# Two transformer blocks on one core: the opening norm's sums, the merged norms' signal, and work moved around waits

## What is computed

```
h = rmsnorm(x)                                   # "mix"
x = x + gated_branch_mixer(h)                    # w_in (6144 columns), conv, layernorm, pool, w_o
x = x + cross_attention(rmsnorm(x), rmsnorm(mem))
x = x + moe(rmsnorm(x))                          # 16 experts, top 2 of one group
x = rmsnorm(x)                                   # "f", end of block 1
for i in (0, 1):
    h = rmsnorm(x) * (1 + sc1) + sh1             # "n" (i = 0), "d" (i = 1)
    x = x + g1 * (nsa_mixer(h) or diff_mixer(h))
    h = rmsnorm(x) * (1 + sc2) + sh2             # "m0", "m1"
    x = x + g2 * (relu(h @ w_mlp_in)**2 @ w_mlp_out)
```

## Time and profile before

| what | value |
|---|---|
| median of 3 runs | 1421.11 us (1421.02 to 1424.01) |
| profiled execution | 1422.67 us, its span 1421.0 us |
| TensorE matmul busy | 1370.0 us, 96%, 10833 records |
| VectorE, ScalarE, GpSimd busy | 958.3, 629.1, 78.5 us |
| mean granted TensorE clock | 0.987 |
| read from HBM | 256.77 MB |

### The profile page before, as it was taken

How to read it: one execution, slowest core, us unless ns; L and a number is a source line. 1 busy time by engine, 2 the same in 40 slices (tenths; PEclk the granted TensorE clock), 3 DMA queues, 4 the chain that set the end, 5 groups by cost and what they waited for, 6 DMA issues and landing times.

```text
span 1421.0 us, 25909 instructions
## 1 busy us (share of the span) xinstructions
PE 1370.0 (96%) x10833; PEld 1306.9 (92%) x10833; DVE 958.3 (67%) x1189; ACT 629.1 (44%) x802; POOL 78.5 (6%) x131
## 2 busy tenths in 40 slices
PE   7999999999999999999999998999999987999998
PEld 6999999898899999999888578999999876999998
DVE  5569886654676767677675867888876675645553
ACT  5434435344443333333456634344445444444442
POOL 4013000000000000010100000000000000000000
PEclk9999999999899999999999999999999999999999
DMA  8565535443368887885451045999964421455551
GB/s 238 178 194 178 183 122 177 141 134 124 99 236 280 265 272 258 280 264 185 134 163 60 2 159 187 311 299 317 312 221 149 129 90 31 134 182 187 178 178 60
DMA packets 172579, 259.00 MB, mean 182 GB/s; under 512 B 5125, under 2 KB 147762, under 8 KB 172498
## 3 DMA queue, kind: packets, MB, share of 16 engines
q1 hardware_dynamic: 160890, 203.13, 44.2%
q0 software_dynamic: 10768, 53.43, 11.2%
q10 hardware_dynamic: 840, 1.28, 0.3%
HBM read 256.77 MB, written 1.05 MB: 181 GB/s over the span
## 4 chain that ended last, share of the span: by engine, by line
PE 83%; DVE 10%; ACT 3%; DMA 2%; issue 2%; ACTq 0%; DVEq 0%
PE ring L681 60%; PE acc L681 22%; DVE w_lo L1789 2%; ACT w_hi L1322 2%; DMA raw<-in_w_in_dram 1%; DVE arena L1933 1%; ACT arena L1322 1%; PE acc L1148 1%; PE ring L965 1%; DMA raw<-in_w_mlp_in_dram 1%; DVE arena L1838 0%; DMA raw<-in_w_xo_dram 0%; DVE norm L1804 0%; DMA raw<-in_diff_w_out_dram 0%; DVE stat L2337 0%
## 5 line engine op out<-in xcount | busy, mean ns | idle before, releaser
L1789 DVE TENSOR_TENSOR w_lo<-raw,w_hi 128x2048 fp32r<-128x2048 f32 (+1 forms) x191 | 437.0, 2290 | 302.4 <-ACT w_hi L1322 301.9
L681 PE MATMUL ring<-h_hi,w_hi 128*128 128x256 f32 x2088 | 602.2, 288 | 7.2 <-DVE h_lo L1853 2.6
L681 PE MATMUL ring<-h_lo,w_hi 128*128 128x256 f32 x2088 | 593.8, 284 | 0.0
L681 PE MATMUL ring<-h_hi,w_lo 128*128 128x256 f32 x2088 | 593.7, 284 | 0.0
L1322 ACT ACTIVATE w_hi<-raw 128x2048 fp32r<-128x2048 f32 (+1 forms) x191 | 363.8, 1905 | 248.6 <-DMA raw<-in_w_mlp_out_dram 70.0
L681 PEld LDWEIGHTS ring<-h_hi,w_hi 128*128 128x128 f32 x2088 | 403.4, 193 | 14.2 <-issue 10.5
L681 PEld LDWEIGHTS ring<-h_lo,w_hi 128*128 128x128 f32 x2088 | 403.5, 193 | 2.5 <-issue 2.2
L681 PEld LDWEIGHTS ring<-h_hi,w_lo 128*128 128x128 f32 x2088 | 403.3, 193 | 0.0
L681 PE MATMUL acc<-e_hi,w_hi 128*128 128x256 f32 x768 | 218.8, 285 | 0.1
L681 PE MATMUL acc<-e_lo,w_hi 128*128 128x256 f32 x768 | 217.4, 283 | 0.0
L681 PE MATMUL acc<-e_hi,w_lo 128*128 128x256 f32 x768 | 217.4, 283 | 0.0
(11 more groups left out here) (286 smaller groups left out, 1273.6 us busy)
## 6 DMA issues: line engine op xcount, KB each, us to landing
arena<-in_w_ada_dram POOLq DMA_DIRECT2D x64, 768.0 KB, 6.1
raw<-in_w_mlp_in_dram SPq DMA_DIRECT2D x32, 1024.0 KB, 5.7
raw<-in_w_mlp_out_dram SPq DMA_DIRECT2D x32, 1024.0 KB, 5.1
raw<-in_w_in_dram SPq DMA_DIRECT2D x24, 1024.0 KB, 5.3
raw<-in_w_e_gate_dram SPq DMA_DIRECT2D x16, 1024.0 KB, 5.6
raw<-in_w_e_up_dram SPq DMA_DIRECT2D x16, 1024.0 KB, 6.3
raw<-in_w_e_down_dram SPq DMA_DIRECT2D x16, 1024.0 KB, 6.4
raw<-in_diff_w_in_dram SPq DMA_DIRECT2D x12, 1024.0 KB, 5.2
```

The lines of the kernel that those rows point to most:

```text
L681: return nc.tensor.matmul(dst, lhs, rhs, start=start, stop=stop, **kw)
L1789: tt(w_lo[q % SPL][:, 0:n], raw[q % RAW][:, 0:n], w_hi[q % SPL][:, 0:n].bitcast(F32), ALU.subtract)\
```

## The change

x is loaded in two halves. ScalarE squares each half on the token rows, 1024 elements a row, with the row's sum from the same instruction; the root and VectorE's reciprocal then work on 128x2. VectorE multiplies the identity by these (two 128x128 diagonals, in blocks of MEM_T), TensorE's ones matrix spreads them over the partitions into acc[0], and VectorE copies that into the norm row. The vectors' transposes go to acc[1], the memory rows' to acc[0] to acc[3], and the ring's plan loses six uses. SyncE issues its nine vector loads between panel 0 and panel 1. ScalarE takes its first table as Sqrt and rounds panel 1 only behind the h blocks.

The norm n stands ahead of f in `NORMS`, with a buffer of its own for its scaled blocks (N_QR), and GpSimd also waits for f's sum. Further: in the last step of the sparse attention n_norm goes ahead of n_pt_odd; VectorE's last `ahead(p + 2)` of an MLP is left out, and made behind the residual in the first; the split of output panel 2 of d_o goes behind the differential attention on both engines; lambda's Exp goes between the value panels; d_out squares before it copies; the Sqrt table and both last splits come before the last d_out; VectorE makes the low parts of d_o's operand between the head scalings, and ScalarE waits for the scaling's own signal instead of a small copy; d_o's first panel goes block by block. Five fillers' counts are changed.

```diff
@@ -236,7 +236,7 @@
...
     first, count, at = {}, {}, 0
-    for name, n in (("x_t", 4), ("mix_stat", 1), ("vecs", 1), ("a_gate", 2), ("mem_t", 4), ("a_val", 2), ("mem_stat", 1),
+    for name, n in (("x_t", 4), ("a_gate", 2), ("a_val", 2), ("mem_stat", 1),
                     ("c_x", 2), ("c_c", 2), ("c_b", 2), ("u_pool", 2), ("gates", 12), ("x_k", 4), ("ln_stat", 1), ("x_v", 2), ("lv_stat", 1),
@@ -267,7 +267,7 @@
...
-        NORMS = ("x", "ffn", "f", "n", "m0", "d", "m1")
+        NORMS = ("x", "ffn", "n", "f", "m0", "d", "m1")
         PER_NORM = {"squared": 4, "summed": 1, "scaled": KB, "hi": KB, "ready": KB}
@@ -472,10 +472,11 @@
...
             x_rows = a["x"][0].rearrange("(t p) n -> p t n", p=P)
-            sp.dma_start(arena[:, 0:2048].rearrange("p (t n) -> p t n", t=2), x_rows).then_inc(S("x_landed"), 16)
-            for p in range(RAW):
-                load_panel(sp, turn, p)
+            for t in range(2):
+                sp.dma_start(flat(0, t * D, D), x_rows[:, t, :]).then_inc(S(f"x_landed{t}"), 16)
+            load_panel(sp, turn, 0)
             vec_loads(sp, VEC_SOURCES(a)[9:])
+            load_panel(sp, turn, 1)
             sp.wait_ge(S("vecs_landed"), 16 * N_VEC_DMA)
@@ -662,6 +663,7 @@
...
             pool.wait_ge(*sig("n_ready", KB))
+            pool.wait_ge(*sig("f_summed", 1))
             for at, pe0 in ((Z_K, 96), (Z_V, 112)):
@@ -797,32 +799,32 @@
...
             pe.wait_ge(S("ident_landed"), 16)
-            def turn_rows(name, at0, sem):
+            def turn_rows(dst, at0, sem):
                 for i in range(4):
-                    f = FL[name] + i
-                    open_fill(f)
                     for b in range(2):
...
                             src = arena[:, at0 + t * D + (2 * i + b) * P:at0 + t * D + (2 * i + b + 1) * P]
-                            last = nc.tensor.transpose(bank(f)[:, b * T + t * P:b * T + (t + 1) * P], src, ident[:])
+                            last = nc.tensor.transpose(dst(i)[:, b * T + t * P:b * T + (t + 1) * P], src, ident[:])
                     last.then_inc(S(sem), 1)
...
             keep_busy(FL["x_t"], 4)
-            pe.wait_ge(S("x_landed"), 16)
-            turn_rows("x_t", 0, "x_turned")
+            for t in range(2):
+                pe.wait_ge(S(f"x_landed{t}"), 16)
+            turn_rows(lambda i: bank(FL["x_t"] + i), 0, "x_turned")
             pe.wait_ge(S("ones_landed"), 16)
-            stats("mix", lambda k: blk(SQ + k)[:, 0], "mix_squared")
-            keep_busy(FL["vecs"], 4)
+            keep_busy(FL["a_gate"], 5)
+            pe.wait_ge(S("mix_diagonal"), 1)
+            for t in range(2):
+                mm(acc[0][:, t * P:(t + 1) * P], ones[:], blk(MEM_T)[:, 0, t * P:(t + 1) * P], True, True)
             pe.wait_ge(S("vecs_landed"), 16 * N_VEC_DMA)
             pe.wait_ge(S("gains_landed"), 16 * 2 * len(GAIN_ROWS))
-            open_fill(FL["vecs"])
             for i, n in enumerate(VEC_PARTS):
-                last = nc.tensor.transpose(bank(FL["vecs"])[:, i * P:i * P + n], vec_in[0:n, i, :], ident[0:n, 0:n])
+                last = nc.tensor.transpose(acc[1][:, i * P:i * P + n], vec_in[0:n, i, :], ident[0:n, 0:n])
             last.then_inc(S("vecs_turned"), 1)
-            keep_busy(FL["a_gate"], 6)
+            keep_busy(FL["a_gate"], 8)
             full("a_gate", split="mix_ready", together=1)
             pe.wait_ge(S("mem_landed"), 16)
-            turn_rows("mem_t", 2048, "mem_turned")
+            turn_rows(lambda i: acc[i], 2048, "mem_turned")
             full("a_val")
@@ -997,7 +999,7 @@
...
-            keep_busy(FL["n_q"], 4)
+            keep_busy(FL["n_q"], 1)
@@ -1299,8 +1301,12 @@
...
             head_spread(FL["s_spread"], (0, 1, 2, 3), D_HEADS, lambda j: bank(FL["s_spread"] + j), "spread_s_spread")
-            keep_busy(FL["d_o"], 3)
-            full("d_o", pairs_ready("so_ready"), norm="m1")
+            keep_busy(FL["d_o"], 5)
+            linear_first([PN["d_o"]], FL["d_o"], pairs_ready("so_ready"))
+            for i in range(1, 4):
+                linear(PN["d_o"] + i, FL["d_o"] + i, KB, 2, lambda k: h_hi[:, k, :], lambda k: h_lo[:, k, :])
+                stat_pair("m1", i - 1)
+            stat_pair("m1", 3)
             mlp(1)
@@ -1383,21 +1389,23 @@
...
             act.wait_ge(S("pads"), 1)
-            func(note[:, 14:15], eps[:], ACT.Square)
-
-            act.wait_ge(S("ones_landed"), 16)
-            squares_of("mix", x_t[:], blk(SQ, 8), lambda j: drained_wait(act, FL["x_t"] + j))
-            root("mix")
+            func(note[:, 14:15], eps[:], ACT.Sqrt)
+            for t in range(2):
+                act.wait_ge(S(f"x_landed{t}"), 16)
+                last = func(blk(SQ + 4 * t, 4), flat(0, t * D, D).rearrange("p (b t) -> p b t", b=4), ACT.Square, accum_out=stat[:, t:t + 1])
+            last.then_inc(S("early_steps"), 1)
+            act.wait_ge(S("early_steps"), 1)
+            func(stat[:, 2:4], stat[:, 0:2], ACT.Sqrt, scale=1.0 / D, bias=eps[:]).then_inc(S("early_steps"), 1)
             ahead(1 - SPL)
+            high_parts("mix", h_hi, blk(SQ, 8))
             ahead(2 - SPL)
-            high_parts("mix", h_hi, blk(SQ, 8))
             ahead(0)
...
             act.wait_ge(S("mix_ready"), KB)
-            squares_of("mem", blk(MEM_T, 8), blk(SQ, 8), lambda j: drained_wait(act, FL["mem_t"] + j))
+            squares_of("mem", blk(MEM_T, 8), blk(SQ, 8), lambda j: act.wait_ge(S("early_steps"), 3 + j))
             ahead(PN["a_val"] + 1)
@@ -1546,7 +1554,7 @@
...
             ahead(PN["n_q"])
-            high_parts("n", h_hi, blk(SQX, 8), lambda b: mods[:, 0, b:b + 1])
+            high_parts("n", h_hi, blk(N_QR, 8), lambda b: mods[:, 0, b:b + 1])
             act.wait_ge(*sig("f_summed", 1))
@@ -1722,7 +1730,8 @@
...
                 vals = blk(D_V, 8).rearrange("p (t c) n -> p t (c n)", t=2)[:, :, i * HID:(i + 1) * HID]
-                ahead(PN["d_v"] + i)
+                if i < 3:
+                    ahead(PN["d_v"] + i)
                 act.wait_ge(S("panel_done"), PN["d_v"] + i + 1)
@@ -1732,8 +1741,11 @@
...
             act.dma_start(flat(D_HEADS, 0, 2 * P), a["k_spread_heads"]).then_inc(S("s_table_landed"), 16)
-            for i in range(1, 4):
-                take_v(i)
+            take_v(1)
+            act.wait_ge(S("lam_dots"), 1)
+            func(lam[:, 0:2], lam[:, 0:2], ACT.Exp).then_inc(S("lam_exp"), 1)
+            take_v(2)
+            take_v(3)
@@ -1745,11 +1757,9 @@
...
                 o = acc[k % 2][:].rearrange("p (b t) -> p b t", b=2)
+                func(blk(SQX + 2 * k, 2), o, ACT.Square).then_inc(S("s_squared"), 1)
                 func(blk(D_Q + 2 * k, 2), o, ACT.Copy).then_inc(S("d_o_out"), 1)
-                func(blk(SQX + 2 * k, 2), o, ACT.Square).then_inc(S("s_squared"), 1)
-
-            act.wait_ge(S("lam_dots"), 1)
-            func(lam[:, 0:2], lam[:, 0:2], ACT.Exp).then_inc(S("lam_exp"), 1)
+
             d_exp(0)
@@ -1760,11 +1770,12 @@
...
                     d_exp(h + 2)
+            func(note[:, 15:16], ones[:, 0:1], ACT.Sqrt)
+            ahead(PN["d_o"])
             d_out(3)
-            ahead(PN["d_o"])
             row_root("s_sums", P)
             for j in range(4):
-                act.wait_ge(S("s_normed"), j + 1)
+                drained_wait(act, FL["s_spread"] + j)
                 func(h_hi[:, 2 * j:2 * j + 2, :], blk(D_Q + 2 * j, 2), ACT.Copy).then_inc(S("so_hi"), 1)
@@ -1860,21 +1871,25 @@
...
                 drains(nc.vector.tensor_copy(x_t[:, 2 * i:2 * i + 2, :].rearrange("p b t -> p (b t)"), bank(f)[:]), f)
-            inverse("mix")
+            dve.wait_ge(S("early_steps"), 2)
+            chain.did(nc.vector.reciprocal(stat[:, 2:4], stat[:, 2:4]))
+            chain.settle()
+            dve.wait_ge(S("ident_landed"), 16)
+            tt(blk(MEM_T).rearrange("p b (t n) -> p (b t) n", t=2), ident[:].unsqueeze(1).to_broadcast([P, 2, P]),
+               stat[:, 2:4].unsqueeze(2).to_broadcast([P, 2, P]), ALU.mult).then_inc(S("mix_diagonal"), 1)
             ahead(1 - SPL)
-            f = FL["vecs"]
             dve.wait_ge(S("vecs_turned"), 1)
             for i, n in enumerate(VEC_PARTS):
-                last = nc.vector.tensor_copy(vec[:, i, 0:n], bank(f)[:, i * P:i * P + n])
-            drains(last, f)
-            drained_wait(dve, FL["vecs"])
+                last = nc.vector.tensor_copy(vec[:, i, 0:n], acc[1][:, i * P:i * P + n])
+            chain.did(last)
+            chain.did(nc.vector.tensor_copy(norm[:, 2, :], acc[0][:, 0:T]))
             drained_wait(dve, FL["x_t"] + 3)
...
             for i in range(4):
-                f = FL["mem_t"] + i
                 dve.wait_ge(S("mem_turned"), i + 1)
-                drains(nc.vector.tensor_copy(blk(MEM_T, 8)[:, 2 * i:2 * i + 2].rearrange("p b t -> p (b t)"), bank(f)[:]), f)
+                nc.vector.tensor_copy(blk(MEM_T, 8)[:, 2 * i:2 * i + 2].rearrange("p b t -> p (b t)"), acc[i][:])\
+                    .then_inc(S("early_steps"), 1)
```

(25 more changed lines are left out.)

## The result

The changed kernel took 1406.15 us (median of four runs, 1403.57 to 1407.99), the kernel before 1422.56 beside it (1421.02 to 1425.92): ratio 0.9883, 95% interval 0.9866 to 0.9900. Over all its eight runs the changed kernel's median is 1405.88. Its profiled execution took 1403.57, span 1401.9: 19.1 less than the span of before, though the medians differ by 16.4 to 17. So this trace is a lucky one by some 2 us.

What follows compares the result with a forecast made beforehand. TensorE works nearly all the time, leaving short gaps at the seams between stages; gains 7.6 + 3.6 + 0.3 + 3.1 + 1.3 = 15.9 from 1422.67 give 1406.8, less 1.56: 1405.2 us, range 1401.5 to 1412.5.

Steps and rivals of the forecast that it cites:

- Part 1: Opening up to the first projection's first matmul: 16.05 instead of 19.71, gain 3.65, of which 2.2 left after panel 1.
- Rival (a): Opening: vectors land no earlier, since short rows and GpSimd's constants share the engines; 1408.6 us, chance 0.13.
- Part 2: Memory rows' transposes in own banks: waits (4.05) and slow stretch (1.7) go; with Part 1 taken as 7.6.
- Part 3: Merged norms: with the order turned round, n's root no longer waits for f's sums; gain 3.6.
- rival (c): Merged norms: something other than the shared counter holds the root, so reordering fails; 1408.8 us, chance 0.05.
- Part 4: End of the first MLP: one panel's low part (2.29) leaves the chain ahead of the residual; gain 0.3.
- Part 7: Last pair of the sparse attention: n_norm(15) goes ahead of a copy; gain 0.
- Part 5: Start of the differential attention: earlier exponentials shrink the scores' wait to 1.8; gain 3.1, or 1.9 if slow stretch stays.
- Part 6: End of the differential attention: last sums 2 us later, reciprocal unmoved, gain behind it 1.3 (2.9 without the slow stretch).
- the lower bound: End of the differential attention: gain 0 if the slow stretch moves into the fillers at 1185.
- Rival (b): Clock at 1.2 GHz at panel 1 (1.7), Part 6 at 0 (1.3), Part 5's stretch stays (1.2); 1409.4, chance 0.13.
- Rival (d): From panel 1's new wait TensorE stays at 1.2 GHz, 4.6 us a panel; five give 1428, slower; chance 0.03.

Runs made afterwards that it cites:

- run 8: Changed kernel with the old order of loads (panel 0, panel 1, then the vectors): 1408.39 us, ratio 0.9883.
- run 2: Kernel before with only the memory rows transposed into the four accumulator banks instead of the ring: 1415.55 us, ratio 0.9947.
- run 4: Kernel before with the differential attention's edits alone, at its start and its end: 1417.60 us, ratio 0.9968.
- run 1: Kernel before with the opening's edits alone (token-row sums, x in two loads, vectors between panels, memory transposes in own banks): 1415.07 us, ratio 0.9942.
- run 7: Changed kernel with panel 1's high part ahead of h's eight high parts on ScalarE again: 1409.95 us, ratio 0.9891.
- run 12: run 11's kernel, but third split early on ScalarE again, VectorE's low part between d_o's last residual and the norm's reciprocal: 1399.74 us, ratio 0.983.
- run 9: Changed kernel with both panel splits of d_o moved from ahead of the last output block to behind the last norm's scalings: 1404.43 us, ratio 0.9867.
- run 10: run 9's kernel with the residual stage's third split also moved behind m1's sums and root: 1408.42 us, ratio 0.9903.
- run 11: run 10's kernel with ScalarE copying vectors and norm row in the opening, and fillers cut there and ahead of d_o: 1408.70 us, ratio 0.9905.
- run 3: Kernel before with the merged norms' edits alone (n before f, own buffer for scaled blocks, one filler instead of four): 1417.08 us, ratio 0.9966.

## Why the prediction was right, and where its steps were not

The time forecast, 1405.2, lies 0.95 below the median and inside the range. The kernel before was taken at 1421.11 and measured 1422.56 beside the changed one; the gain was forecast as 15.9 and is 16.4 between the medians. But the sum was of edits alone, and in the trace those gave 14.5, less 0.7 at w_o, so 2.1 too little; the rest of the trace's 19.1, 5.3, is time won in untouched code where less clock was lost, and about 2 of it is the luck of this execution. The means of all executions say the same: of the 15.9 the forecast had 2.9 from the clock (1.7 and 1.2) and 13.0 from waits, measured are 6.0 and 11.1. **The step that is missing is the clock outside the edited places, put at nothing without a reason.** Two errors of 2 to 3 us, of opposite sign, nearly cancelled, and that is luck.

**Part 1 failed in a size.** It had the first matmul at 16.05; it came at 17.70 (17.23 in the second trace). The failed step is "its high part can start at about 9.4": panel 0 had landed only by 10.91, ScalarE waited 1.32 for it, and all that follows (low part, copies, scaling) kept its distances. The kernel before used that panel only at 13.33, so none of its rows shows the landing, and the step took the end of the root for it. The vectors came at 13.76 (12.47 and 14.16 in other traces), not 12, and did not bind: VectorE's copies waited for its own low part until 15.06. At panel 1 the wait was 1.82 as worked out, but with the later start only 0.64 of the 2.2 was left. The two squares took 2.18 with their accumulator reads, against 2.4 taken.

**Rival (a)** is refuted by run 8: with the loads in the old order the vectors came at 16.57, with the new at 12.5 to 14.2. The rule of the Trainium skill, "DMA: Bandwidth & Descriptors", Bandwidth, that transfers under 64 KB are dominated by descriptors, may hold for their rate, which no run here isolates; it did not set their landing.

**Part 2 was right**, and run 2 isolates it: 6.0 against 5.75 reckoned (4.05 and 1.7). Parts 1 and 2 together gave 6.6 of 7.6: Part 1 fell 1.6 short of its 2.2, and Part 2 gave 0.6 more than the 5.4 that the joint sum left for it.

**Part 3 was right**: 3.45 alone, 3.46 in the change, 3.6 forecast; rival (c) falls. **Part 4**: 0.75 against 0.3, of which the wait of 0.26 is seen; a slow stretch lies across the first fixed point, so the rest isn't resolved. **Part 7**: nothing, as said.

**Part 5** named two values, 3.1 and 1.9, by whether the slow stretch stays. Both occur with the same wait of 1.77: 1.93 in the changed kernel, 3.55 in run 4. The step that failed is the reason for the choice, "the single gap of 2.30 before 685.03 left the clock at 2.4 GHz, so I count the 1.2 us as won": a gap's length did not decide it. And the stretch is worth 1.7 in lost clock, not 1.2. The Exp table's load stands well ahead now, at 1119.42. The Sqrt table's, at the end of the stage, is 1.28 again (the instruction before it ends at 1162.16, it starts at 1162.17, the next one at 1163.47), so the switch of about 2.66 with a drain that the Trainium skill, "ScalarE: Activation LUTs", What ACT_TABLE_LOAD costs, gives is not seen here.

**Part 6** was right in its chain and off in its size: 1.72 against 1.3. The new gap came (2.97 for 3.2), the reciprocal started where it was put (17.54 earlier, against 17.36 for the stage), and the slow stretch moved into the fillers, 4.23 for twelve, as the lower bound had it. That held the spread 1.5 longer than the reciprocal did (1173.28, 16.02 earlier), and still the part won, since d_o's first panel then ran at full clock: the lower bound, 0, charged the fillers' slowness without crediting the panel. **Rival (b)** happened in two of its three places; the other untouched places outweighed it. **Rival (d)** did not: no trace lost more than 5.1 in one stretch.

The 0.7 at w_o is a landing: ScalarE waited 2.92 for a w_o panel instead of 1.65, with two high parts of h queued behind it (first row before, second row after):

```profile
255.50 1.91 ACT L1322 ACTIVATE w_hi<-raw 128x2048 fp32r<-128x2048 f32 x1 [1.65 <-DMA raw<-in_w_o_dram]
250.15 1.91 ACT L1328 ACTIVATE w_hi<-raw 128x2048 fp32r<-128x2048 f32 x1 [2.92 <-DMA raw<-in_w_o_dram]
```

The loss is there in the second trace of the changed kernel (1.7) and in runs 1, 7 and 12 (1.5 to 1.7), absent in runs 8 to 11 with the same or nearly the same opening, and absent in all five traces with the old order of the opening (both of before, runs 2, 3 and 4). So an execution of the changed kernel need not have it; whether the new opening makes it likelier stays open.

## What to carry to other kernels

Give a side computation banks of its own before anything cleverer: four spare banks won 6 of the opening's 6.6. When a split is moved off a waiting chain, follow the buffer that it releases to the load behind it; the same move brought a wait of 4.48 (run 11) or none (run 12) by where the low part came to stand, and the place that works is the idle time of its own engine just before the chain's next step. And before a gain in one trace is put down to an edit, subtract what the granted clock lost in each stretch, look at a second trace, and compare the mean granted clock of all executions.

## What the runs showed of the hardware

The clock's fall to 1.2 GHz is not a fixed answer to a given gap: behind the same wait of 1.82 at panel 1 it stayed up in both traces of the changed kernel and in run 12, and fell in runs 1, 9, 10 and 11, and the kernel before, unaltered, lost 19.8 and 23.1 in two traces, the changed one 11.9 and 15.2. On average over all executions the changed kernel still loses less, 14.2 against 20.2. Every loss was 1.7 us or a multiple, up to 5.1, but for those that the end of the trace cut off. The runs of one kernel spread over 2 to 8 us, as wide as most parts of this change, and for the changed kernel the clock is most of that: its eight times lie within 4.6 of each other, within 2.0 once each one's lost clock is taken off. For the kernel before, taking it off does not narrow the spread, so there more than the clock is in it. What the clock goes by within those traces stays open.

Landings move too: the transposes of x began at 6.54, 7.08 and 7.33 with one load (both of before, run 2) and at 7.27, 6.56 and 6.99 with two (both of the changed kernel, run 1), so the later start of the transposes in the changed kernel is not the price of halving it.
